# The adaLN modulation made by VectorE beside attention and the MLP, in place of TensorE beside the opening and the projection

## The reference

```python
cond_x = jax.nn.silu(c)[:, None, :]
cond_c = jax.nn.silu(c_ctx)
...
    mx = jnp.split(cond_x @ ada_w[i] + ada_b[i], 6, axis=-1)
    mc = jnp.split(cond_c @ ada_w[i] + ada_b[i], 6, axis=-1)
    hx = modulate(rms_norm(x, g[0]), mx[0], mx[1])
    hc = modulate(rms_norm(ctx, g[0]), mc[0], mc[1])
...
    x = x + mx[2] * rms_norm(ox, g[1])
    x = x + mx[5] * rms_norm(sq_relu_mlp(modulate(rms_norm(x, g[2]), mx[3], mx[4]),
                                         ff_w1[i], ff_w2[i]), g[3])
```

## Time and profile before

| | us |
|---|---|
| median of 3 runs (3452.32 to 3454.87) | 3454.66 |
| span of the profiled execution | 3457.7 |
| TensorE busy in it | 3317.7 |
| VectorE / ScalarE / GpSimd busy | 1818.6 / 1291.3 / 691.5 |

### The profile page before, as it was taken

One profiled execution on the slowest core, in us unless ns is written; L12 is line 12 of the kernel. 1 busy time (PEld: TensorE's weight loads), 2 busy tenths in 40 slices (PEclk: granted clock), 3 DMA queues, 4 the chain that ended last, 5 costly groups with the idle time before them and its releaser, 6 DMA issues. The chain is left out here.

```text
span 3457.7 us, 39533 instructions
## 1 busy us (share of the span) xinstructions
PE 3317.7 (96%) x15472; PEld 2443.2 (71%) x15472; DVE 1818.6 (53%) x2304; ACT 1291.3 (37%) x2118; POOL 691.5 (20%) x383
## 2 busy tenths in 40 slices
PE   6999999999999999999999999898999999999998
PEld 3666444555788888888889878652456788888886
DVE  3233544433555544554586444588576654445444
ACT  4333344445553333333454223452113532233332
POOL 0000478667331101300120100110011320002001
PEclk8999999999999999999999999999999999999999
DMA  8753533321253333433465311102513333333333
GB/s 329 290 214 103 179 65 77 77 61 48 98 171 127 112 97 97 146 98 96 131 195 175 113 62 39 51 1 101 203 49 109 132 126 97 98 98 117 121 98 104
DMA packets 134552, 406.62 MB, mean 118 GB/s; under 512 B 24153, under 2 KB 38265, under 8 KB 130016
## 3 DMA queue, kind: packets, MB, share of 16 engines
q1 hardware_dynamic: 134368, 404.11, 36.1%
HBM read 345.05 MB, written 58.92 MB: 117 GB/s over the span
## 5 line engine op out<-in xcount | busy, mean ns | idle before, releaser
L1598 PE MATMUL psum<-hid_high,w_high_and_low 128*128 128x512 f32 (+1 forms) x1536 | 416.3, 356 | 11.7 <-DVE hid_low L1831 9.4
L1581 PE MATMUL psum<-h_high,w_high_and_low 128*128 128x512 f32 (+1 forms) x1536 | 415.6, 356 | 0.7 <-DVE w_high_and_low L1741 0.7
L1648 ACT ACTIVATE w_high_and_low<-w_raw 128x1024 fp32r<-128x1024 f32 x226 | 238.6, 1056 | 342.3 <-PE psum L1598 238.8
L1853 POOL TENSOR_TENSOR squares_then_rstd_of_out<-squares_then_rstd_of_out,square_out 128x512 f32<-128x512 f32 (+1 forms) x69 | 103.2, 1495 | 1277.1 <-ACT square_out L1663 1277.1
L1741 DVE TENSOR_TENSOR w_high_and_low<-w_raw,w_high_and_low 128x1024 fp32r<-128x1024 f32 x226 | 285.7, 1265 | 90.9 <-ACT w_high_and_low L1648 90.2
L1313 POOL TENSOR_TENSOR probs_added<-probs_added,probs_turned 128x1024 f32<-128x1024 f32 x128 | 308.1, 2407 | 66.6 <-ACT probs_turned L1238 54.0
L1598 PEld LDWEIGHTS psum<-hid_high,w_high_and_low 128*128 128x128 f32 x1536 | 274.2, 190 | 54.5 <-DVE hid_low L1831 7.8
L1581 PEld LDWEIGHTS psum<-h_high,w_high_and_low 128*128 128x128 f32 x1536 | 273.1, 189 | 42.5 <-DVE w_high_and_low L1741 1.3
L1280 DVE TENSOR_REDUCE row_max<-psum 128x1 f32<-128x1280 f32 x120 | 179.0, 1492 | 228.5 <-PE psum L1176 137.2
L1828 DVE TENSOR_TENSOR hid_high<-hid_relu_and_square 128x512 fp32r<-128x512 f32 (+1 forms) x160 | 111.5, 697 | 351.3 <-ACT hid_relu_and_square L1731 351.2
L1598 PE MATMUL psum<-hid_low,w_high_and_low 128*128 128x512 f32 (+1 forms) x768 | 272.2, 354 | 0.0
(11 more groups left out here) (472 smaller groups left out, 6713.0 us busy)
## 6 DMA issues: line engine op xcount, KB each, us to landing
w_raw<-in_ff_w_dram SPq DMA_DIRECT2D x320, 512.0 KB, 3.6
ada_ring<-in_ada_w_dram SPq DMA_DIRECT2D x24, 2048.0 KB, 9.8
w_raw<-in_w_out_dram SPq DMA_DIRECT2D x38, 512.0 KB, 3.5
scratch_spectra<-spectrum_out SPq DMA_DIRECT2D x32, 256.0 KB, 2.0
filter_ring<-scratch_spectra SPq DMA_DIRECT2D x16, 512.0 KB, 3.9
stream_in<-scratch_x SPq DMA_DIRECT2D x27, 256.0 KB, 4.4
w_raw<-in_w_hy_dram SPq DMA_DIRECT2D x12, 512.0 KB, 3.9
scratch_hyena<-mixed SPq DMA_DIRECT2D x12, 512.0 KB, 2.6
```

What stands on the lines that cost most here:

```text
L1581: mm = pe.matmul(bank[:, 0:n], x[i % SLOTS][:, k, :], y[:, k, a:a + n], start=(k == 0 and m == 0), stop=(k == KT - 1 and m == 2))
L1598: mm = pe.matmul(bank[:, 0:n], x[i % SLOTS][:, 2 * k + half, :], y[:, k, 0:n], start=(k == 0 and m == 0), stop=(k == HT - 1 and m == 2))
L1648: act.activation(w_hi[i % SLOTS], raw[i % 2], ACT.Copy).then_inc(w_rounded, 1)
L1853: pool.tensor_tensor(acc_out[:, q % 2, 0:n], acc_out[:, q % 2, 0:n], sq_out[:, v % 2, 0:n], ALU.add).then_inc(added_out, 1)
```

## The change

Four pieces stay as they are (layer 0's scale and shift of the mixer). Their ring has four slots now and so holds all of them, and the opening's ScalarE stream is interleaved anew: one square of the next chunk, one shift of this one. The other 20 pieces are made in another way, by ModulationRows: VectorE multiplies 128 rows of a piece by the conditioning of their features (one scalar a partition) and adds them up over the 8 k tiles in SBUF, for each stream apart, and TensorE only sums the 128 partitions at the end of a batch of 32 such additions (add_up, with a matrix of ones) and turns the sums. Attention has six batches (layer 0's other pieces, layer 1's shift and scale of the mixer, both streams; 192 additions), the MLP of layer 0 two (layer 1's other pieces, latent stream alone; 64 additions). The rows come as granules of 0.25 MB, in a ring of 3 in attention and 2 in the MLP. The additions of batch b are spread evenly over the slots between two sums (ADA_SUMS: slot 19 of pairs 1 to 6). The sums use the bank of the rows and of the exponentials' sums (ROW_BANK), so rows_of and sums_of now also wait for the batch's bias. In the MLP they take a bank of the ring of six.

```diff
-    SLOTS = 3
+    SLOTS = 4
 
     def __init__(self, nc, g, d, mem, sems, pieces, banks):
-        self.g, self.w_in, self.order, self.banks = g, sems[:3], pieces, banks
-        self.sel_in, self.made, self.copied, self.turned, self.biased, self.folded = sems[3:]
+        self.g, self.w_in, self.order, self.banks = g, sems[:4], pieces, banks
+        self.sel_in, self.made, self.copied, self.turned, self.biased, self.folded = sems[4:]
...
-ADA_FIRST = [(0, piece) for piece in (2, 3, 0, 1, 4, 5, 6, 7, 8, 9)]
-ADA_LATER = [(0, piece) for piece in (10, 11)] + [(1, piece) for piece in range(ADA_PIECES)]
+ADA_FIRST = [(0, piece) for piece in (2, 3, 0, 1)]
+BOTH, LATENT = (0, 1), (0,)
+ADA_IN_ATTENTION = [(0, (4, 5), BOTH), (0, (6, 7), BOTH), (0, (8, 9), BOTH), (0, (10, 11), BOTH)] + [(1, (2, 3), BOTH), (1, (0, 1), BOTH)]
+ADA_IN_MLP = [(1, (4, 5, 6, 7), LATENT), (1, (8, 9, 10, 11), LATENT)]
+
+
+class ModulationRows:
+
+
+    def __init__(self, nc, g, d, mem, sems, batches, slots):
+        self.g, self.src, self.batches, self.slots = g, d["ada_w"], batches, slots
+        self.w_in, (self.stepped, self.summed, self.copied, self.turned, self.biased, self.folded) = sems[:slots], sems[slots:]
+        self.w, self.total = tile(nc, mem, "ada_rows_in", [P, slots, BANK]), tile(nc, mem, "ada_rows_added", [P, 4, BANK])
...
+    def load(self, sp, m):
+        b, piece, k = self.granules[m]
+        if m >= self.slots:
+            sp.wait_ge(self.stepped, self.rows_by[m - self.slots])
+        sp.dma_start(self.w[:, m % self.slots, :], self.src[self.batches[b][0] * ADA_PIECES + piece][:, k, :]).then_inc(self.w_in[m % self.slots], 16)
+
+    def add(self, dve, r):
+        m, s = self.rows[r]
+        b, piece, k = self.granules[m]
+        layer, pieces, streams = self.batches[b]
+        w, scale = self.w[:, m % self.slots, :], self.g.cond[:, k, s:s + 1]
+        total = self.total[:, pieces.index(piece) * len(streams) + s, :]
+        if s == streams[0]:
+            dve.wait_ge(self.w_in[m % self.slots], 16 * (m // self.slots + 1))
+        if k == 0:
+            if b:
+                dve.wait_ge(self.summed, b)
+            dve.tensor_scalar(total, w, scale, None, ALU.mult).then_inc(self.stepped, 1)
+        else:
+            dve.wait_ge(self.stepped, self.row_no[m - 1, s] + 1)
+            dve.scalar_tensor_tensor(out=total, in0=w, scalar=scale, in1=total, op0=ALU.mult, op1=ALU.add).then_inc(self.stepped, 1)
+
+    def add_up(self, pe, b, bank):
+        pe.wait_ge(self.stepped, self.batch_rows[b])
+        for x in range(4):
+            mm = pe.matmul(bank[32 * x:32 * x + 32, :], self.g.ones[:, 0:32], self.total[:, x, :], start=True, stop=True, tile_position=(0, 32 * x))
+        mm.then_inc(self.summed, 1)
+
+    def copy(self, act, b, bank):
+        act.wait_ge(self.summed, b + 1)
+        if b:
+            act.wait_ge(self.turned, b)
+        act.activation(self.sums[:], bank, ACT.Copy).then_inc(self.copied, 1)
+
+    def turn(self, pe, b, bank):
+        pe.wait_ge(self.copied, b + 1)
+        for m in range(BANK // P):
+            mm = pe.matmul(bank[:, 4 * m:4 * m + 4], self.sums[:, m * P:(m + 1) * P], self.g.ident[:, 0:P:32], start=True, stop=True)
+        mm.then_inc(self.turned, 1)
...
-        AFTER = {6: 4, 9: 5, 12: 6, 15: 7, 18: 8, 21: 9}
...
-                for i in range(NEEDED, A):
-                    ada.load(sp, i)
...
-                for i in range(NEEDED, A):
-                    ada.multiply(pe, i)
-                    ada.turn(pe, i)
-                    if i == NEEDED:
-                        add_squares(2)
+                add_squares(2)
...
-                of_x(1)
-                shift(0, range(0, 4))
+                shift(0, (0, 1))
+                for k in range(KT):
+                    of_x(1, (k,))
+                    if k + 2 < KT:
+                        shift(0, (k + 2,))
                 root(1)
-                shift(0, range(4, KT))
-                of_x(2)
-                shift(1, range(0, 4))
+                for k in range(KT):
+                    of_x(2, (k,))
+                    shift(1, (k,))
                 root(2)
-                shift(1, range(4, KT))
...
-                    ada.load(sp, u + 1 + ada.SLOTS)
...
-                    ada.turn(pe, step - 1)
-                    ada.multiply(pe, step)
...
-                    ada.copy(act, step - 1)
...
-                    ada.bias(dve, step - 1)
...
+    ADA_SUMS = [CYCLE * pair + 19 for pair in range(1, 7)]
...
+        ada_rows_at, granules_at = {}, {}
+        for b, at in enumerate(ADA_SUMS):
+            calm = range(ADA_SUMS[b - 1] + 1 if b else 2, at)
+            for x in range(32):
+                ada_rows_at.setdefault(calm[x * len(calm) // 32], []).append(32 * b + x)
+        for m in range(len(ada.granules)):
+            done = ada.rows_by[m - ada.slots] - 1 if m >= ada.slots else None
+            granules_at.setdefault(START if done is None else min(i for i in ada_rows_at if ada_rows_at[i][-1] >= done) + 1, []).append(m)
...
+                    for m in granules_at.get(i, ()):
+                        ada.load(sp, m)
...
+                    if i in ADA_SUMS:
+                        pe.wait_ge(row_copied, rows_until(i - 1))
+                        pe.wait_ge(logged, sums_until(i - 1))
+                        ada.add_up(pe, ADA_SUMS.index(i), ada_bank)
+                    if i - 2 in ADA_SUMS:
+                        ada.turn(pe, ADA_SUMS.index(i - 2), ada_bank)
...
+                    if i - 3 in ADA_SUMS:
+                        ada.bias(dve, ADA_SUMS.index(i - 3), ada_bank)
+                    for r in ada_rows_at.get(i, ()):
+                        ada.add(dve, r)
...
+    norm_beside = [(0, 3), (KT + 1, KT + 5), (26, 35), (46, 55), (88, 96), (99, 108), (152, 300)]
+    calm = [i for i in range(N) if not any(a <= i < b for a, b in norm_beside) and (steps[i][1] is None or steps[i][2] != HT - 1)]
+    rows_at, sums_at, at, r = {}, {}, 0, 0
+    for b, (of_layer, of_pieces, streams) in enumerate(ADA):
+        left = list(range(r, r + 32))
+        r += len(left)
+        while left:
+            take = 2 if len(streams) == 2 else 1
+            rows_at[calm[at]], left = left[:take], left[take:]
+            at += 1
+        sums_at[calm[at]] = b
+        at += 1
...
+                    if i - 1 in sums_at:
+                        ada.turn(pe, sums_at[i - 1], bank_of(i - 1))
+                    if i in sums_at:
+                        bank_for(unit_of[i, "ada"])
+                        ada.add_up(pe, sums_at[i], bank_of(i))
...
+                    for r in rows_at.get(i, ()):
+                        ada.add(dve, r)
```

More of the change, by code:

```diff
@@ L1332, in out_and_mlp @@
     N = len(steps)
[L1333 removed]
+    ADA = ADA_IN_MLP if ada_d else []
+    norm_beside = [(0, 3), (KT + 1, KT + 5), (26, 35), (46, 55), (88, 96), (99, 108), (152, 300)]
[10 more added lines that the diff above has]
+        at += 1
+    units = []
+    for i, (c, e, j) in enumerate(steps):
+        units += [(i, half) for half in range(1 if e is None or (c is not None and j < HT) else 2)]
+        if i in sums_at:
+            units.append((i, "ada"))
     unit_of = {x: u for u, x in enumerate(units)}
[L1335 removed]
+    made_by = [sum(1 for i, half in units[:u + 1] if half != "ada") for u in range(len(units))]
+    through = [made_by[unit_of.get((i, 1), unit_of[i, 0])] for i in range(N)]
     def kind(i):
@@ L1339, in kind @@
         return "next" if c is None else "out" if e is None else "up" if j < HT else "down"
-    released = {"out": 0, "up": 0, "down": 0, "next": 0}
+    released = {"out": 0, "up": 0, "down": 0, "next": 0, "ada": 0}
     release = []
     for i, half in units:
-        released[kind(i)] += 1
-        release.append((kind(i), released[kind(i)]))
+        what = "ada" if half == "ada" else kind(i)
+        released[what] += 1
+        release.append((what, released[what]))
     def at_step(c, e, j):
```

116 lines of the change are left out of this document (84 added, 32 removed).

## The result

The changed kernel takes 3529.77 us (median of 4 runs, 3527.30 to 3545.65) against 3454.76 (4 runs, 3452.32 to 3456.30) in the same rounds: 1.0226 times as long, interval 1.0205 to 1.0247. The profiled execution is the slowest of the four: 3545.65 us, its span 3543.9, 86.2 more than the span of before. An execution's time is some 1.8 us longer than its span, so the profiled execution of before, with a span of 3457.7, took an estimated 3459.5 us, 5 more than the median. By the medians the change costs 75.0 us. A second profile, further down, has a span 68.0 us above that of before.

What follows compares the result with a forecast made beforehand. TensorE, busy 3317.7 of 3457.7 us, was taken to bound the kernel. Terms -53 + 13 + 5 + 42 + 31 + 7 + 25 = +70 us on the median 3454.7 gave 3525 us, range 3422 to 3570.

Steps and rivals of the forecast that it cites:

- Opening: Opening: VectorE starts at 34.9 us as before and ends at 68 against 81.2; saves 13 us.
- Projection: Projection: fourteen pieces of 3.15 us leave TensorE's path, 44 us, less 4 for chains less covered; saves 40 us.
- TensorE's batches in attention: Attention: six batches of four 32-row matmuls and four turns, 2.2 us each on TensorE; +13 us.
- MLP: MLP: two batches cost TensorE 4 us, and 64 additions beside its products 1 us; +5 us.
- Stalls by additions in attention: Attention: additions wait for GpSimd at the SBUF port, delaying maxima: 42, 31 and 7 us, and 25 at batch ends.
- TensorE's waits for the end of a batch: Attention: TensorE waits for a batch's last four additions, 4.5 us for five batches, 2.5 for batch 0; 25 us.
- some 85: Attention: a sign, that pairs grow from 56 and 66 us to about this many us.
- Its own range: Whole kernel: the main forecast alone, chance 0.6, spans 3480 to 3570 us, stall terms at two thirds and one and a half.
- Rival 3: Attention: worst stalls hold throughout, ends cost 6 us each, clock falls to some 0.92 (+30); 3585 us, chance 0.08.
- arithmetic of a double slot: Attention: port waits add 2.8 us to each double slot in the first four pairs, 1.4 in the last four.
- rival 1: Attention: additions find the port free as GpSimd's idle time moves beside them, stalls below 35 us; 3425 us, chance 0.22.
- Rival 2: Attention: VectorE keeps the port over two additions, stalls and ends 32 us in all; 3452 us, chance 0.1.

Runs made afterwards that it cites:

- second profile: The changed kernel once more, unaltered, for another profile; 3527.47 us, span 3525.7.
- kernel without additions: Changed kernel with each of attention's 192 additions replaced by a memset of 128x1, that modulation left out; 3426.86 us, ratio 0.9913.
- halved GpSimd operations: Changed kernel with GpSimd adding the two heads' probabilities in two operations of 512 columns, not one of 1024; 3491.27 us, ratio 1.0106.
- 96 wide additions: Changed kernel with two pieces of a batch added per operation of 1024 columns in attention, 96 additions in place of 192; 3451.92 us, ratio 0.9988.
- 192 reductions: Changed kernel with each of attention's additions replaced by a maximum over the same rows, one column written, that modulation left out; 3430.37 us, ratio 0.9923.
- Both together: Changed kernel with attention's additions 1024 columns wide (96) and GpSimd's additions in two operations of 512 columns; 3447.26 us, ratio 0.9967.
- The cheapest place: Against the kernel before: layer 0's pieces stay on TensorE, all of layer 1's go to VectorE in layer 0's MLP; 3431.88 us, ratio 0.9934.

## Why the prediction came out

The time, 3529.77 us, is 5 us from the forecast of 3525, and the mechanism is the one it named: the savings are real, and additions that wait beside GpSimd make the maxima late. That the sum came so close is in part luck, since errors in its terms cancel. The terms, measured in the first profile:

| Term | Forecast | Measured, from |
|---|---|---|
| Opening | -13 | -11.9, end at 69.3 (68 named) |
| Projection | -40 | -46.8, the rest of 58.7 |
| TensorE's batches in attention | +13 | +13.9, groups of the kernel without additions |
| MLP | +5 | -0.6 for the tail, -0.1 for layer 0's MLP alone; the tail of the other kernels with two batches there -0.2 to +5.5 |
| Stalls by additions in attention | +105 | +121.8 (637.6 - 515.8); +102.6 in the second profile |
| Of these, TensorE's waits for the end of a batch | +25 | 8.6 (3 waits) |
| Not in the sum: other cost of attention without additions | 0 | +11 (25.0 - 13.9) |

The measured terms make -58.7 + 13.9 + 11.1 + 121.8 - 0.6 = +87.5, and 1.3 us more were gained between the first key and attention: the 86.2 of the spans. The second profile has the same stalls at +102.6 and a total of +68.0. The medians, +75.0, lie between the two.

The projection lost the pieces' whole 3.15 us and a little more: fourteen of them are 44, so the 4 us allowed for chains less covered were not needed. VectorE did not start at 34.9 us in the opening, as the forecast had it, but at 37.8: the fourth piece's bias came at 37.72, before at 34.78. The loads were put at nothing: in attention VectorE waited for a granule three times, 8.4 us in all, each time ahead of a maximum. The pairs came out close to the "some 85", at 75 to 88 us.

Two sums of the forecast do not come out as written. Its own range, the stall terms at two thirds and at one and a half, is 3490 to 3577, not 3480 to 3570. Rival 3's terms are 125 us, or 132 with batch 0's 7, not 130, and 130 on 3457 is 3587. The 5.06 us of GpSimd stand in no row named there; the earlier trace rows have 4.87. None of this bears on the outcome.

Two steps of the forecast were wrong in kind, and hid each other. First, its stalls are all waiting. In fact, against the kernel without additions, TensorE waits 88.4 - 15.6 = 72.8 us more and is *busy* 549.2 - 500.2 = 49.0 us longer (31.3 in the second profile), with the same 2206 instructions. The matmuls are slower in the mean: the group of the values,

```profile
L1231 PE MATMUL psum<-probs_turned,v_pair 128*64 128x512 f32 x640 | 176.1, 676 | 0.0
```

against the same group without additions,

```profile
L1235 PE MATMUL psum<-probs_turned,v_pair 128*64 128x512 f32 x640 | 159.0, 618 | 0.0
```

took 676 and 618 ns in the mean. The granted clock was 0.85 and 0.94 in the two pairs shown above, time at its upper level (2.4 GHz) mixed with time at the lower (1.2). In the earlier trace rows, with TensorE busy 263 of 268 us, it is 1.00. One such stretch stands behind a wait for a maximum:

```profile
377.28 0.39 PE L1270 MATMUL psum<-identity,row_max 128*8 128x128 f32 x2 [2.21 <-DVE row_max L1370]
377.59 0.63 PE L1218 MATMUL psum<-q_other,k_high 128*128 128x512 f32 x1
```

From 374.0 to 377.2 us TensorE was busy 1.06 us. From 377.2 to 384.7 the granted clock was 0.54, and such a matmul took 0.63 us; then the clock was 1.00 again, and from 389.75 it took 0.40. Not every wait brings this: behind the one of 1.66 us that ends at 432.61 the clock stayed at 1.00. The forecast knew this loss, at a clock of 0.92, but put it into rival 3 alone, where it belonged into the main sum. Rival 3's price of 30 us for it would have been about right (31 to 49).

Second, the arithmetic of a double slot went too far: "7.9" and "7.2 to 7.85" us for every double slot with rankings. TensorE waited for maxima in single stretches (up to 5.2 us), and between them additions and GpSimd's operations missed one another: half of the additions lasted 1.03 us or less in the first profile (1.43 in the second), where the forecast had 1.5 to 2.9. GpSimd idles once TensorE slips: ahead of its running additions in attention it was idle 149.2 us in all, before the change 66.6. The waiting came out at 73 us, not 105, and the ends of batches at 8.6 of it, not 25. That is what rival 1 argued with, but far from its 35 us. Rival 2, VectorE keeping the port over two additions, is refuted by the halved GpSimd operations, where both of two additions waited.

The forecast did not see that waits count by number, and steeply. 96 wide additions cost 25 us and 192 narrow ones 103. The reading that fits, which is argued and not shown by itself: with one addition in a gap of 1.2 us, its wait is mostly slack; with a second in the same gap, the maximum behind is late.

The lock itself was told with the Trainium skill ("SBUF — State Buffer", Who interferes with whom). The same section says that a VectorE instruction with at most one SBUF input outside the two-port modes does not contend: by that rule the trace agrees, 192 reductions of 669 to 686 ns beside GpSimd at work.

## What to carry to other kernels

Before work goes onto an engine that "is idle half of the time", look at what it shares. By the clock VectorE's gaps of 0.9 and 1.2 us nearly held three additions of 0.69; with GpSimd at the port for 4.87 of 5.11 us they held one. Count operations at such a port, not their microseconds: fewer and wider operations cost 25 us here in place of 103, and shorter ones on the other side 64, for the same work. Both together gained only 5 us over the wide ones. The cheapest place was layer 0's MLP, where GpSimd is busy 168.7 of 1032.2 us. And charge TensorE's idle stretches twice, as waiting and for the slower clock after them: here 73 us and another 31 to 49.

## What the runs showed of the hardware

- A VectorE operation on 128x512 with two SBUF inputs takes 0.73 us alone and up to 2.92 beside GpSimd's 128x1024 additions. With 128x512 ones it takes at most 1.87, and 256 columns instead of 512 still take up to 2.65. The wait is at most one GpSimd operation less what it has run, up to 2.2 or 1.1 us, whatever VectorE's own length: 1024 columns take 1.27 us alone and up to 3.43.
- The two engines take turns: GpSimd's 1.27 us became 1.72 and 1.54 beside two VectorE additions of 1.72 each.
- The first operation of each sum has one SBUF input and one scalar, takes 0.47 us alone, less than two thirds of the others, and is held up too, up to 2.56 us in the changed kernel. The reduction with one SBUF input, 0.68 us, never is; it writes one column, the other 512.
- Two executions of the changed kernel had the same idle time in attention (88.4 and 86.9 us), but TensorE was busy 549.2 us in one and 531.5 in the other. Why the clock fell lower in the first stays open.
